# Memory attentions: VectorE subtracts a turned part one step later, behind the next unit's maximum and normalising

## The chip, the cores and the metric

The kernel runs on one core of a Trainium2 chip. Its time is the device time of one execution in microseconds (us), and a change is judged by the medians of several executions. Five engines work side by side, each through its own list of instructions in order: TensorE (PE in the profile; its weight loads are PEld), VectorE (DVE), ScalarE (ACT), GpSimd (POOL) and SyncE (SP). They wait for each other through semaphores.

## The reference

Two transformer blocks on 512 tokens of width 1024. Each of the three layers in them ends with a memory cross attention, which is what the change touches, and a feed-forward part:

```python
def memory_cross_attention(h, m, wq, wkv, wo):
    q = (h @ wq).reshape(b, t, XA_HEADS, XA_HEAD_DIM)          # 4 heads of 256
    k, v = jnp.split(m @ wkv, 2, axis=-1)                      # 256 memory rows
    ...
    s = jnp.einsum("bthd,bmhd->bhtm", q, k).astype(jnp.float32) * (XA_HEAD_DIM ** -0.5)
    p = jax.nn.softmax(s, axis=-1).astype(v.dtype)
    o = jnp.einsum("bhtm,bmhd->bthd", p, v).reshape(b, t, D_MODEL)
    return o @ wo
```

In the first block the same attention stands once, after a mixer of two causal attentions; in the second block it stands once after each of two mixers. That makes three memory attentions: `xa0`, `xa1` and `xa2`.

## The kernel before

All large products are made from float32 operands split in two: a high part (`_hi`, rounded) and the rest (`_lo`, the value less its high part), and a product is three matmuls, high by high, low by high and high by low (L974). ScalarE makes the high parts of activations, VectorE the rests; for weights, GpSimd makes most rests (L820).

A memory attention has 16 **units**: 4 heads by 4 query tiles of 128 tokens, numbered 0 to 15. The work on unit s is spread over the engines:

- TensorE: scores S(s), four float32 matmuls into a bank of the ring `ps_s` (L1381).
- VectorE: the negated row maximum of the scores (L2710, reads `ps_s`).
- ScalarE: the exponential with its row sum (L1975).
- VectorE: reciprocal of the sum (L2486) and the normalising multiply (L2488).
- TensorE: two transposes of the normalised tile, T(s), into a bank of the ring `ps_l` (L1123).
- ScalarE: the high part of the turned tile (L1967). VectorE: its **rest** (L2725), which needs the turned tile and the high part, and gives the bank back.
- TensorE: when a head's four units are turned, its values product in two halves, V(h,0) and V(h,1), six matmuls each (L974 on `vm_hi`). ScalarE takes the high part of the result (L1981), VectorE its rest (L2716), here called P(h,0) and P(h,1).

The order is written out once, by `attention_events`, as a list of events that all engines walk; each takes of it what is its own. In step s stand S(s), then at some steps P, then T(s-3), and V(h,0) at the end of step 4h+8, V(h,1) at the end of step 4h+10. P(h,0) and P(h,1) stand in steps 4h+9 and 4h+11. On VectorE the function `walk` follows the list: at S(s) it makes the maximum of s and then normalises s-1 (at S(15) both 14 and 15), and at T(s-3) it makes the rest of s-3.

What TensorE waits for here: T(s) waits until s is normalised; V(h,·) waits for the rest of unit 4h+3 (`wait_read` on the turned group); and every group of the ring `ps_l` (T and V alike) waits until the group four places earlier has been given back, by a rest or by a P. The order of those groups is T0 to T5, V(0,0), T6, T7, V(0,1), T8, T9, V(1,0), T10, T11, V(1,1), T12, T13, V(2,0), T14, T15, V(2,1), V(3,0), V(3,1).

Of the kernel before, what the change touches and what calls it, by code (L numbers as in the profile page):

```python
# [2 lines left out]

# [14 lines left out]
T = 512  # L18
# [474 lines left out]
def build(nc, A, out):  # L493
    plan = make_plan()
    L, S = plan.L, plan.S
# [17 lines left out]
    def weight(name):  # L513
        name, _, layer = name.partition(":")
        a = A[name]
        return a[int(layer or 0)] if len(a.shape) == 3 else a

    with ExitStack() as ctx:
# [255 lines left out]
        def out_group(t, half):  # L774

            return (L, L.base["ffn1_last"] + t) if half else (S, S.base["out"] + t)
# [193 lines left out]
        def _(pe):  # L970
# [253 lines left out]
            def causal_values(name, rows, vt):  # L1224
                at = plan.events[name][1]

                def values(g, h, _):
                    claim(pe, L, g)
                    wait_read(pe, L, at["T", h, TT - 1])
                    for k in range(TT):  # L1230
                        ins = pe.matmul(bank(L, g)[rows(h), k * P:T], vt(h, k), pt(h)[:, k, k * P:T],
                                        start=k == 0, stop=k == TT - 1)
                    ins.then_inc(l_full, 1)
                return values
# [15 lines left out]
            def pair_values(name, vt):  # L1250
                at = plan.events[name][1]

                def values(g, p, _):
                    claim(pe, L, g)
                    wait_read(pe, L, at["T", p, TT - 1] + 1)
                    for k in range(TT):
                        for e in (0, 1):
                            ins = pe.matmul(bank(L, g)[64 * e:64 * e + 64, k * P:T], vt(2 * p + e, k), pt_row(e, k),  # L1258
                                            start=k == 0, stop=k == TT - 1)
                    ins.then_inc(l_full, 1)  # L1260
                return values
# [1010 lines left out]
        def _(dve):  # L2272
# [74 lines left out]
            for n in range(KD):  # L2347
                g = S.base["x_in"] + n
# [9 lines left out]
            g = S.base["vecs"]  # L2358
# [4 lines left out]
            g = S.base["table"]  # L2363
# [24 lines left out]
            g = S.base["forget"]  # L2388
# [15 lines left out]
            g = S.base["flip"]  # L2404
# [3 lines left out]
            g = S.base["cum"]  # L2408
# [31 lines left out]
            for kind, h, i in ev:  # L2440
                g = at[kind, h, i]
# [36 lines left out]
            def ring_who(g):  # L2478
                return L.who[g]

            def plain_norm(name, exp_done, buf, width, h, i):

                u = TT * h + i
                exp_done(h, i)
                a = u % 8
                step(dve.reciprocal(rl[:, a:a + 1], ls[:, a:a + 1]))  # L2486
                sync()
                dve.tensor_scalar(buf[:, i, 0:width(i)], buf[:, i, 0:width(i)], rl[:, a:a + 1], None, ALU.mult)\  # L2488
                    .then_inc(u_p, 1)

            def walk(name, heads, scores, exp_done, buf, width, values, filled=None, turned=None):
                ev, at = plan.events[name]
                seen, normed = 0, 0
                for kind, h, i in ev:
                    g = at[kind, h, i]
                    upto = normed
                    if kind == "S":
                        scores(g, h, i)
                        upto = seen
                        seen += 1  # L2500
                        if seen == heads * TT:
                            upto = seen
                    done = kind == "G" and ring_who(g) == "v" and h[2] == h[3] - 1
                    if done:
                        upto = seen
                    while normed < upto:
                        plain_norm(name, exp_done, buf, width, *divmod(normed, TT))
                        normed += 1
                    if done:
                        filled(g, *h[0:2])  # L2510
                    if kind == "T" and turned:
                        turned(g, h, i)
                    if kind == "P":
                        values(g, h, i)


            def pair_norm(exp_done, p, i):
# [81 lines left out]
            for n in range(KD):  # L2599
                g = L.base["proj_b"] + n  # L2600
# [88 lines left out]
            def cross(c, k_norm, after):  # L2689
# [29 lines left out]
                def turned_rest(g, h, i):  # L2719
# [6 lines left out]
                        .then_inc(l_free["v"], 1)  # L2726

                walk(name, XA_HEADS, scores, lambda h, i: wait_read(dve, S, at["S", h, i]), p_x, lambda i: MEM, values,
                     turned=turned_rest)
                residual(L.base[f"xo{c}"], after, *([angle_steps()] if c == 1 else []))  # L2730
# [63 lines left out]
            g = S.base["norm4"]  # L2794
# [88 lines left out]
            for q in range(4):  # L2883
                g = L.base["pool_w"] + q
# [19 lines left out]
            g = S.base["ln_mean"]  # L2904
# [128 lines left out]
            g = L.base["dq2"] + 1  # L3033
# [27 lines left out]
            for half in (0, 1):  # L3061
                for j in (0, 1) if not half else (1,):
                    query_turn(half, j)
                g = L.base[f"uk{half}"]
# [20 lines left out]
                for kind, h, i in plan.events[name][0]:  # L3085
                    g = at[kind, h, i]
# [23 lines left out]
            for t in range(TT):  # L3110
# [3 lines left out]
                for half in (0, 1):  # L3114
                    ring, g = out_group(t, half)
# [45 lines left out]
```

## Time and profile before

| | |
|---|---|
| median of 3 runs | 2370.75 us (2370.62 to 2371.77) |
| profiled execution, its own time | 2372.24 us |
| its span on the core | 2370.4 us |
| TensorE busy | 2331.8 us, 98% of the span |
| VectorE busy | 1224.9 us, 52% |
| ScalarE busy | 944.9 us, 40% |
| GpSimd busy | 994.8 us, 42% |

The profile page gives busy times of one execution; the span is what the trace covers. TensorE is nearly always at work, so a microsecond in which it waits is a microsecond of the kernel, wherever it lies. The three memory attentions are 33 us each.

### The profile page before, as it was taken

Reading aid. Unit: us, or ns where it says so; the run is one execution under the profiler, and the core shown is the slowest. Engines: PE = TensorE matmul, PEld = TensorE weight load, DVE = VectorE, ACT = ScalarE, POOL = GpSimd, SP = SyncE. Lnnn points to the kernel's source line nnn. Section 1 sums busy time; section 2 is a strip of 40 time slices with the busy share of each in tenths; the row PEclk is TensorE's granted clock in tenths of the full one; section 3 lists DMA queues with packets and bytes.
Section 4 is the critical chain, followed back from the end, with each engine's and each line's share of the span. In section 5 each row is a group of like instructions: output and inputs, shape, how many; then the busy total and the mean of one; then the engine's idle time right before and its main releaser. Section 6 shows DMA issues by size and latency. Waiting matters only on the chain.

```text
span 2370.4 us, 29903 instructions
## 1 busy us (share of the span) xinstructions
PE 2331.8 (98%) x11132; PEld 1863.8 (79%) x11132; DVE 1224.9 (52%) x2017; ACT 944.9 (40%) x1451; POOL 994.8 (42%) x744
## 2 busy tenths in 40 slices
PE   8999999999999999999999999999999999999999
PEld 6777778878888888857878888887667878888887
DVE  4454546343433436794466555556774343655544
ACT  3345444433332226535344222225875433322222
POOL 4323335223545445535515545444113233545443
PEclk9999999999999999999999999999999999999999
DMA  5222222422232323223222232322013422232231
GB/s 175 71 72 93 92 90 89 160 72 87 96 106 90 103 92 107 90 72 107 71 69 96 93 103 90 101 93 77 29 37 107 160 72 73 97 107 89 88 107 71
DMA packets 170090, 218.74 MB, mean 92 GB/s; under 512 B 6585, under 2 KB 144107, under 8 KB 169975
## 3 DMA queue, kind: packets, MB, share of 16 engines
q1 hardware_dynamic: 168278, 214.59, 27.6%
q10 hardware_dynamic: 1696, 2.61, 0.3%
q8 instruction: 74, 1.21, 0.2%
q14 instruction: 42, 0.34, 0.0%
HBM read 215.05 MB, written 2.12 MB: 92 GB/s over the span
## 4 chain that ended last, share of the span: by engine, by line
PE 88%; DVE 5%; ACT 3%; issue 2%; DMA 1%; POOL 1%; DVEq 0%; SPq 0%; ACTq 0%
PE ps_l L974 81%; PE ps_s L1493 1%; PE ps_l L1123 1%; ACT w_hi L1649 1%; DVE small L3090 1%; POOL w_lo L820 1%; DVE arena L3082 1%; DVE a_lo L2725 1%; DVE small L2710 1%; PE ps_s L1275 0%; PE ps_s L1322 0%; PE ps_s L974 0%; PE ps_l L1622 0%; DVE small L3092 0%; PE ps_l L1258 0%
## 5 line engine op out<-in xcount | busy, mean ns | idle before, releaser
L820 POOL TENSOR_TENSOR w_lo<-w_raw,w_hi 128x512 fp32r<-128x512 f32 (+1 forms) x740 | 994.6, 1376 | 1354.4 <-ACT w_hi L1649 1344.2
L974 PE MATMUL ps_l<-a_hi,w_hi 128*128 128x512 f32 x1936 | 761.6, 393 | 3.7 <-POOL w_lo L820 2.7
L974 PE MATMUL ps_l<-a_lo,w_hi 128*128 128x512 f32 x1952 | 758.9, 389 | 0.0
L974 PE MATMUL ps_l<-a_hi,w_lo 128*128 128x512 f32 x1936 | 754.4, 390 | 0.0
L1649 ACT ACTIVATE w_hi<-w_raw 128x2048 fp32r<-128x2048 f32 (+2 forms) x196 | 370.6, 1891 | 583.0 <-PE ps_l L974 564.7
L974 PEld LDWEIGHTS ps_l<-a_hi,w_hi 128*128 128x128 f32 x1936 | 363.0, 188 | 89.2 <-issue 9.4
L974 PEld LDWEIGHTS ps_l<-a_lo,w_hi 128*128 128x128 f32 x1952 | 366.2, 188 | 77.6 <-issue 2.2
L974 PEld LDWEIGHTS ps_l<-a_hi,w_lo 128*128 128x128 f32 x1936 | 363.1, 188 | 76.9
L974 PE MATMUL ps_l<-b_hi,w_hi 128*128 128x512 f32 (+1 forms) x892 | 329.5, 369 | 5.8 <-issue 2.3
L974 PE MATMUL ps_l<-b_hi,w_lo 128*128 128x512 f32 (+1 forms) x892 | 326.7, 366 | 0.0
L974 PE MATMUL ps_l<-b_lo,w_hi 128*128 128x512 f32 (+1 forms) x892 | 326.7, 366 | 0.0
L974 PEld LDWEIGHTS ps_l<-b_hi,w_hi 128*128 128x128 f32 x892 | 168.1, 189 | 37.0 <-issue 3.9
L974 PEld LDWEIGHTS ps_l<-b_hi,w_lo 128*128 128x128 f32 x892 | 168.2, 189 | 27.4
L974 PEld LDWEIGHTS ps_l<-b_lo,w_hi 128*128 128x128 f32 x892 | 168.2, 189 | 27.2 <-issue 0.2
L2975 DVE TENSOR_TENSOR x_T<-ps_l,x_T 128x512 f32<-128x512 f32 x160 | 109.2, 688 | 44.6 <-PE ps_l L974 42.6
L2769 DVE TENSOR_TENSOR x_T<-ps_l,x_T 128x512 f32<-128x512 f32 x120 | 82.9, 690 | 59.0 <-PE ps_l L974 58.0
L1681 ACT ACTIVATE a_hi<-x_T,cols 128x512 fp32r<-128x512 f32 x64 | 46.2, 723 | 141.5 <-DVE x_T L2658 141.5
L2658 DVE TENSOR_TENSOR x_T<-ps_l,x_T 128x512 f32<-128x512 f32 x64 | 43.5, 687 | 111.6 <-PE ps_l L974 111.2
L2940 DVE TENSOR_TENSOR arena<-ps_l,rst 128x512 f32<-128x512 f32 x44 | 30.4, 692 | 134.3 <-PE ps_l L974 121.2
L2745 DVE SCALAR_TENSOR_TENSOR arena<-ps_l,rst 128x512 f32<-128x512 f32 x32 | 22.0, 691 | 146.6 <-PE ps_l L974 137.3
L2949 DVE SCALAR_TENSOR_TENSOR arena<-arena,cols 128x512 f32<-128x512 f32 x88 | 91.3, 1038 | 8.4 <-DVE arena L2945 0.3
L2958 DVE TENSOR_TENSOR arena<-ps_l,rst 128x512 f32<-128x512 f32 x44 | 30.3, 691 | 125.9 <-PE ps_l L974 125.9
(314 smaller groups left out, 2446.3 us busy)
## 6 DMA issues: line engine op xcount, KB each, us to landing
w_raw<-in_ffn_w_up_dram SPq DMA_DIRECT2D x44, 1024.0 KB, 5.0
w_raw<-in_w_dram SPq DMA_DIRECT2D x32, 1024.0 KB, 5.1
w_raw<-in_ffn_w_down_dram SPq DMA_DIRECT2D x22, 1024.0 KB, 4.9
w_raw<-in_w_in_dram SPq DMA_DIRECT2D x20, 1024.0 KB, 5.3
w_raw<-in_xa_wkv_dram SPq DMA_DIRECT2D x16, 1024.0 KB, 5.3
w_raw<-in_w_kv_mem_dram SPq DMA_DIRECT2D x8, 1024.0 KB, 5.4
w_raw<-in_xa_wq_dram SPq DMA_DIRECT2D x8, 1024.0 KB, 5.0
w_raw<-in_xa_wo_dram SPq DMA_DIRECT2D x8, 1024.0 KB, 5.1
```

Source lines behind the costliest of these rows:

```text
L820: e.tensor_tensor(w_lo[:, b % 2, o], w_raw[:, b % 2, o], w_hi[:, b % 2, o].bitcast(F32), ALU.subtract).then_inc(w_lo_made[by], 1)
L974: ins = pe.matmul(o, *((v, w) if swap else (w, v)), start=first and n == 0, stop=last and n == 2)
L1123: return pe.transpose(o, v, ident)
L1493: ins = pe.matmul(bank(S, g + swapped)[out:out + 64, :], diag(n, j - first)[rows, :], gl[rows, q, j:j + T], start=j < first + 2, stop=j >= ...
L1649: act.activation(w_hi[:, b % 2, 0:size], w_raw[:, b % 2, 0:size], ACT.Copy).then_inc(w_hi_made, 1)
L1681: act.activation(z_of(k)[0][:, n, :], x[:, n, :], ACT.Copy, scale=gain(k, n)).then_inc(n_hi, 1)
L2658: dve.tensor_tensor(x[:, n, :], bank(L, g)[:, :], x[:, n, :], ALU.add).then_inc(l_free["v"], 1)
L2769: dve.tensor_tensor(x[:, n, :], bank(L, g + n)[:, :], x[:, n, :], ALU.add)\
L2940: dve.tensor_tensor(gp[:, c, 2:T + 2], bank(L, g + c)[:, :], rst, ALU.mult)\
L2949: dve.scalar_tensor_tensor(out=cv[:, c, :], in0=gp[:, c, j:T + j], scalar=wcol(cw + 22 * j, k, i), in1=cv[:, c, :], op0=ALU.mult, op1=ALU. ...
L2958: dve.tensor_tensor(f32[:, c, :], bank(L, g + 2 + c)[:, :], rst, ALU.mult)\
L2975: dve.tensor_tensor(x[:, n, :], bank(L, g + n)[:, :], x[:, n, :], ALU.add)\
```

## The change

`walk` no longer makes the rest of a turned part where T stands in the list. It puts it in a queue and makes it at the next S, behind that unit's maximum and the normalising, or, where no S comes, ahead of the next P or T. Only the memory attentions hand `turned` to `walk`; nothing else moves, and no other engine's list changes.

```diff
+import collections
...
                 seen, normed = 0, 0
+                waiting = collections.deque()
                 for kind, h, i in ev:
...
                     if done:
                         filled(g, *h[0:2])
-                    if kind == "T" and turned:
-                        turned(g, h, i)
+                    while waiting and (kind == "S" or kind in "PT" and waiting[0][0] < g):
+                        turned(*waiting.popleft())
                     if kind == "P":
                         values(g, h, i)
+                    if kind == "T" and turned:
+                        waiting.append((g, h, i))
+                while waiting:
+                    turned(*waiting.popleft())
```

In the changed kernel the lines of `walk`'s parts have other numbers: maximum L2716, reciprocal L2487, normalising L2489, rest L2731, P L2722.

VectorE at the first rest of `xa0`, before (rest of unit 0 into bank `ps_l0`, between the normalising of unit 2 and the maximum of unit 4):

```order
L2710 TENSOR_REDUCE small<-ps_s 128x1
L2486 RECIPROCAL small<-small 128x1
L2488 TENSOR_SCALAR arena<-arena,small 128x256
L2725 TENSOR_TENSOR a2_lo<-ps_l0,a2_hi 128x2x128
L2710 TENSOR_REDUCE small<-ps_s 128x1
L2486 RECIPROCAL small<-small 128x1
L2488 TENSOR_SCALAR arena<-arena,small 128x256
L2725 TENSOR_TENSOR a2_lo<-ps_l1,a2_hi 128x2x128
```

and the same place in the changed kernel:

```order
L2716 TENSOR_REDUCE small<-ps_s 128x1
L2487 RECIPROCAL small<-small 128x1
L2489 TENSOR_SCALAR arena<-arena,small 128x256
L2716 TENSOR_REDUCE small<-ps_s 128x1
L2487 RECIPROCAL small<-small 128x1
L2489 TENSOR_SCALAR arena<-arena,small 128x256
L2731 TENSOR_TENSOR a2_lo<-ps_l0,a2_hi 128x2x128
```

The rest of unit 0 now stands behind the maximum of unit 4 and the normalising of unit 3, and so does each later rest behind one more maximum and normalising.

VectorE at the last scores of `xa0`, before (from the rest of unit 11 in `ps_l2` on, with the maximum of unit 15, the normalising of 14 and 15, and P(1,1) in `ps_l3`):

```order
L2725 TENSOR_TENSOR a2_lo<-ps_l2,a2_hi 128x2x128
L2710 TENSOR_REDUCE small<-ps_s 128x1
L2486 RECIPROCAL small<-small 128x1
L2488 TENSOR_SCALAR arena<-arena,small 128x256
L2486 RECIPROCAL small<-small 128x1
L2488 TENSOR_SCALAR arena<-arena,small 128x256
L2716 TENSOR_TENSOR a_lo<-ps_l3,a_hi 128x512
L2725 TENSOR_TENSOR a2_lo<-ps_l0,a2_hi 128x2x128
L2725 TENSOR_TENSOR a2_lo<-ps_l1,a2_hi 128x2x128
```

and in the changed kernel:

```order
L2716 TENSOR_REDUCE small<-ps_s 128x1
L2487 RECIPROCAL small<-small 128x1
L2489 TENSOR_SCALAR arena<-arena,small 128x256
L2487 RECIPROCAL small<-small 128x1
L2489 TENSOR_SCALAR arena<-arena,small 128x256
L2731 TENSOR_TENSOR a2_lo<-ps_l2,a2_hi 128x2x128
L2722 TENSOR_TENSOR a_lo<-ps_l3,a_hi 128x512
L2731 TENSOR_TENSOR a2_lo<-ps_l0,a2_hi 128x2x128
L2731 TENSOR_TENSOR a2_lo<-ps_l1,a2_hi 128x2x128
```

The rest of unit 11, for which V(2,0) waits, has moved behind the maximum of unit 15 and two normalisings; from P(1,1) on the list is the same.

## Rows read from the trace of the kernel before

**Rows 1.** The page: shares of the chain of work that ended last

```profile
PE 88%; DVE 5%; ACT 3%; issue 2%; DMA 1%; POOL 1%; DVEq 0%; SPq 0%; ACTq 0%
```

**Rows 2.** Windows: the first attention, length, busy time by engine, then granted clock

```profile
499.00:532.00 33.00, 30.75 (x146) 23.68 (x145) 24.86 (x72) 19.05 (x56) 5.09 (x4) 1.00 0.14 48
```

**Rows 3.** Timeline of one turn of VectorE's loop: start, duration, engine; idle before

```profile
509.26 0.41 DVE L2710 TENSOR_REDUCE small<-ps_s 128x1 f32<-128x256 f32 x1
...
509.71 0.47 ACT L1975 ACTIVATE arena<-ps_s,small 128x256 f32<-128x256 f32 x1 [0.89 <-DVE small L2710]
509.78 0.35 DVE L2488 TENSOR_SCALAR arena<-arena,small 128x256 f32<-128x256 f32 x1
...
510.18 0.37 ACT L1967 ACTIVATE a_hi<-ps_l 128x256 fp32r<-128x256 f32 x1
...
510.65 0.42 DVE L2725 TENSOR_TENSOR a_lo<-ps_l,a_hi 128x256 fp32r<-128x256 f32 x1 [0.52 <-ACT a_hi L1967]
510.99 0.41 DVE L2710 TENSOR_REDUCE small<-ps_s 128x1 f32<-128x256 f32 x1
...
511.13 0.50 PE L974 MATMUL ps_l<-a_hi,vm_hi 128*128 128x512 f32 x1 [0.44 <-DVE a_lo L2725]
```

**Rows 4.** Timeline of the attention's start: TensorE, GpSimd and VectorE

```profile
499.22 3.61 PE L1381 MATMUL ps_s<-arena 128*128 128x256 f32 x16
...
500.28 0.42 DVE L2710 TENSOR_REDUCE small<-ps_s 128x1 f32<-128x256 f32 x1 [0.17 <-PE ps_s L1381]
...
501.46 5.09 POOL L820 TENSOR_TENSOR w_lo<-w_raw,w_hi 128x512 fp32r<-128x512 f32 x4 [5.53 <-ACT w_hi L1649]
...
504.59 0.84 DVE L2488 TENSOR_SCALAR arena<-arena,small 128x256 f32<-128x256 f32 x1
...
506.32 0.38 DVE L2488 TENSOR_SCALAR arena<-arena,small 128x256 f32<-128x256 f32 x1
```

**Rows 5.** Timeline of TensorE between the first two halves of values

```profile
512.62 1.02 PE L1381 MATMUL ps_s<-arena 128*128 128x256 f32 x4
...
514.57 0.38 PE L1123 MATMUL ps_l<-keep,arena 128*128 128x128 f32 x2
514.71 0.47 PE L974 MATMUL ps_l<-a_hi,vm_hi 128*128 128x512 f32 x1
```

**Rows 6.** Timeline of the attention's end, TensorE

```profile
523.28 1.02 PE L1381 MATMUL ps_s<-arena 128*128 128x256 f32 x4
...
525.08 0.47 PE L974 MATMUL ps_l<-a_hi,vm_hi 128*128 128x512 f32 x1 [0.34 <-DVE a_lo L2725]
...
527.11 0.77 PE L1123 MATMUL ps_l<-keep,arena 128*128 128x128 f32 x4 [0.39 <-DVE a_lo L2716]
527.86 0.47 PE L974 MATMUL ps_l<-a_hi,vm_hi 128*128 128x512 f32 x1
...
529.32 0.39 PE L974 MATMUL ps_l<-a_hi,vm_hi 128*128 128x512 f32 x1
```

**Rows 7.** Timeline of the attention's end, VectorE

```profile
524.51 0.42 DVE L2725 TENSOR_TENSOR a_lo<-ps_l,a_hi 128x256 fp32r<-128x256 f32 x1 [0.52 <-ACT a_hi L1967]
...
526.10 0.35 DVE L2488 TENSOR_SCALAR arena<-arena,small 128x256 f32<-128x256 f32 x1
526.37 0.68 DVE L2716 TENSOR_TENSOR a_lo<-ps_l,a_hi 128x512 fp32r<-128x512 f32 x1
526.97 0.74 DVE L2725 TENSOR_TENSOR a_lo<-ps_l,a_hi 128x256 fp32r<-128x256 f32 x2
```

**Rows 8.** Timeline of the attention's end, ScalarE

```profile
525.30 0.48 ACT L1975 ACTIVATE arena<-ps_s,small 128x256 f32<-128x256 f32 x1 [0.41 <-DVE small L2710]
...
526.75 0.60 ACT L1981 ACTIVATE a_hi<-ps_l 128x512 fp32r<-128x512 f32 x1 [0.33 <-PE ps_l L974]
```

**Rows 9.** Waits of TensorE in the first attention: us in total, times, longest

```profile
PE ps_l L1123 <- DVE arena L2488: 1.1, 3, 0.5
PE ps_l L974 <- DVE a_lo L2725: 0.8, 2, 0.4
```

## The prediction

> **What bounds the kernel now.** I read the page first: 88% of the chain that ended last runs through TensorE, and 5% through VectorE [rows 1]. So the question is only whether TensorE waits less or more inside the three memory attentions. The windows show the first as 33 us with 30.75 us of TensorE's work, at a granted clock of 1.00 [rows 2]; the other two have the same length, the same clock and TensorE busy to within 0.1 us of it. I therefore work out one attention, on the first one's times, and multiply by three.
>
> The timeline of one turn shows what the change aims at. VectorE's maximum starts at 509.26; the exponential behind it 0.45 later, at 509.71; the turned tile's high part 0.47 later, at 510.18; the rest 0.47 later, at 510.65; and the next maximum 0.34 later, at 510.99 [rows 3]. That is a ring of 1.73 us through two engines, and in it VectorE stands idle for 0.52 us ahead of each rest, since ScalarE makes the exponential of the new unit before the high part of the old one. The change opens this ring: the maximum no longer stands behind the rest.
>
> Is this ring what holds TensorE? Only at the attention's start. From the first values product on, two steps of TensorE are scores, turn, scores, turn and half a values product. The row of scores at 512.62 leads to the turn at 514.57 and the next values at 514.71, and V(0,0) itself took from 511.13 to 512.62 [rows 3, 5]: 1.49 + 2.09 = 3.58 us, without a wait, against 2 x 1.73 = 3.46 us for VectorE. TensorE is the slower of the two there. Its waits by the view of waits are 1.1 us for the normalising and 0.8 for rests [rows 9], and the one of 0.39 for P(1,1) [rows 6], 2.3 us in all.
>
> **The change, part by part.** No instruction is added or taken away; 16 rests in each attention move. From the starts in the rows I take these steps of VectorE: maximum to normalising 0.52 (509.26 to 509.78), normalising to the next instruction 0.27 (526.10 to 526.37), rest to the next 0.34, P to the next 0.60 (526.37 to 526.97) [rows 3, 7]. A step without P is then 0.52 + 0.27 + 0.34 = 1.13 us, if nothing is waited for. From the start of a rest to the matmul that waits for it I have two values: 0.48 (510.65 to 511.13) and 0.57 (524.51 to 525.08) [rows 3, 6, 7].
>
> *Term 1, the start, up to V(0,0).* The first place where order matters is the maximum of unit 4. The normalising of unit 2 starts at 504.59 and takes 0.84 us instead of 0.35 [rows 3, 4]; it ends at 505.43. Now the maximum of 4 can start 0.08 before that end (0.35 against a step of 0.27), at 505.35, and the normalising of unit 3 at 505.87. GpSimd is then still in the last of its four L820 instructions (501.46 + 5.09 = 506.55) [rows 4]. The normalising that started at 506.32 took 0.38 and ended 0.15 after GpSimd; the one at 504.59 ended about as long after the third of the four. I take it that the multiply is held until GpSimd's instruction ends, so from 505.87 it lasts to 506.70, just as before. The Trainium skill says the same of the cause, in the "GPSIMD Engine Reference", section "8. Key points": GpSimd shares its SBUF interfaces with VectorE, and they contend when VectorE runs in a two-port mode. The rows carry the number without it.
>
> From there VectorE is free of the ring: rest 0 at 506.62, maxima of 5, 6 and 7 at 506.96, 508.09 and 509.22, then the rest of unit 3 at 509.22 + 0.52 + 0.27 = 510.01. V(0,0) waits for that rest. In the old kernel the rest of unit 3 stood one step earlier in the list, which is why a ring of 1.73 shortened to 1.13 over three steps doesn't give all of 1.8 us. V(0,0) starts 0.48 later, at 510.49, where it was 511.13: **0.64 us gained**. T(4) and T(5) come earlier too but don't set this. If the multiply is not held, it takes 0.35, and V(0,0) comes 0.48 sooner still: 1.12 gained. That is the bound on the other side. With 0.57 instead of 0.48 it is 0.55.
>
> *Term 2, V(0,1), V(1,0) and V(1,1).* With the ring open VectorE catches up with TensorE and waits for its scores. That makes each half of values depend on something new. V(0,1) needs bank and rest of unit 5, V(1,0) the rest of 7, V(1,1) the bank of unit 9; each of these rests now stands in VectorE's step behind the scores that TensorE made just before. From the first row of scores to the maximum that waits for them is 1.06 us (499.22 to 500.28) [rows 4], then 0.52 + 0.27 to the rest, then 0.57 to the matmul: 2.42 us after the scores began. TensorE by itself would be there after 2.09 [rows 5]. So **each of the three waits 0.33 us: 0.99 lost**. With 0.48 it would be 0.24 each, 0.72. The P's between don't add: in their steps they stand behind the rest.
>
> *Term 3, the end.* I count from the start of S(15), 523.28 before. V(2,0) needs the rest of unit 11. It stood ahead of the maximum of 15 and now stands behind the normalising of both 14 and 15, which waits for the exponential of 15. Maximum at 1.06, exponential at 1.51, normalising of 15 at 2.31 (525.30 to 526.10 is 0.80), rest of 11 at 2.58, V(2,0) at 3.15 [rows 3, 4, 7, 8]. Before: 525.08 - 523.28 = 1.80 [rows 6]. That is 1.35 late. Some of it comes back. T(14) used to wait for P(1,1) and started 2.03 after V(2,0); free of waits it follows after 1.46, as V(3,0) follows V(2,1) (527.86 to 529.32). V(2,1) used to start 0.75 after T(14), and without its wait it needs two turns, about 0.37. So V(2,1) is at 3.15 + 1.46 + 0.37 = 4.98, where it was 4.58. V(3,0) needs the rest of unit 15. This now comes out of another queue: P(2,0) stands ahead of it, and waits for ScalarE's high part of V(2,0), which starts 1.67 after V(2,0) (525.08 to 526.75) and takes 0.60 and about 0.10 more until the reader starts [rows 6, 8]. P(2,0) is at 3.15 + 1.67 + 0.70 = 5.52, the two rests behind it at 6.12 and 6.44, and V(3,0) at 7.01. Before it was 6.04: **0.97 lost**. With 0.48 both times it is 0.79.
>
> Sum for one attention: -0.64 + 0.99 + 0.97 = +1.32 us; three times is +4.0. Against the profiled execution that is 2372.24 + 4.0 = 2376.2; this execution lay 1.5 above the median of the runs, so I put it on the median: 2370.75 + 4.0 = 2374.7. Behind V(3,0) nothing is left that could take it up: TensorE goes on into the output product without a wait [rows 6], and the weights' next parts are asked for when TensorE is done with older ones, so they move along.
>
> The bounds: with the multiply not held and 0.48 throughout, -1.12 + 0.72 + 0.79 = +0.39, or +1.2 in all (2371.9). With 0.57 everywhere -0.55 + 0.99 + 0.97 = +1.41, or +4.2 (2375.0).
>
> **The rivals.** I call 0.2% (4.7 us) what a measurement of this kernel can tell from no change.
>
> *Faster.* The ring is the first thing that one sees, and 0.52 us of VectorE's idle time in each turn of it goes [rows 3]. TensorE's waits that could go with it are 2.3 us in one attention [rows 6, 9]; if all went it would be -6.9 us, 2363.9. The Trainium skill speaks for this: "Perfetto Trace Analysis", section "Optimization Strategies", advises to speed up the engines that block TensorE where it waits. By that rule the ring would be the thing to cut and the time would fall. What speaks against it in this kernel is that two of the three kinds of wait are for rests and for a P, that is, for what the change puts later, and that the ring isn't the slower one from V(0,0) on. It decides only if term 3 doesn't come: that is, if V(2,0) didn't need the rest of 11. Its own wait row says it does [rows 6]. Chance 0.07 for more than 4.7 us.
>
> *Slower by over 0.2%.* Term 2's lag is longer than I take it. It is put together from a maximum at the attention's start and a release at its end, and it counts three times in each attention. At 0.26 us above the sum, +1.58 in each attention, the bound is passed; that is 0.09 more for each of the three halves. If VectorE, waking from a wait, takes 0.2 more each time, it is 1.32 + 0.60 = 1.92, +5.8, 2376.5. Nothing in the rows shows such a waking time, but nothing bounds it well either. Chance 0.28.
>
> *The gains pay for the losses.* The multiply isn't held, so that term 1 gives 1.12, and terms 2 and 3 lie near their low ends: +1 to +2 us, 2372.3. It is the low half of my own case.
>
> **How the numbers follow.** Slower by something up to 0.2% is my forecast, with 0.65 for the whole band within 0.2%, nearly all of it on the slow side. Faster 0.07, slower 0.28. The forecast of the likeliest case is 2374.7. For the range, the low end is the case in which gains pay, 1.2, with 0.3 for what runs scatter: 2371.6. The high end is the slow rival's 2376.5.
>
> **What would show it.** V(0,0) at about 11.3 us from the attention's first scores instead of 11.9. No idle time of VectorE ahead of its rests, but before its maxima, waiting for scores. A wait of 0.2 to 0.35 us ahead of V(0,1), V(1,0), V(1,1) on the rest. The longest wait of each attention ahead of V(2,0), 1.7 us by this working, where it was 0.34 in the row [rows 6]; the wait for P(1,1) gone; and a new one of 0.5 us ahead of V(3,0). The exponential and normalising keep their durations. I am wrong if V(2,0) starts less than 2.5 us after S(15), if V(0,0) gains over 1.5 us, or if TensorE's granted clock falls below 1.00 behind the longer wait.

## The result and the profile after

The changed kernel takes **2379.02 us** in the median of 10 runs (2374.81 to 2379.92), the kernel before, run beside it on the same chip, 2371.81 (10 runs, 2370.62 to 2373.09). The ratio is 1.0027, with a 95% interval of 1.0018 to 1.0035: slower, by 7.2 us where 4.0 were forecast, and above the top of the range (2376.5). Two things have to be told apart from here on. The span of the profiled execution grew by 4.0 us (2370.4 to 2374.4), the number that was forecast, though in part by chance, as is shown below; the timed median grew by more. In what follows two executions that were disturbed as a whole, one of e18 (9963 us) and one of the kernel before beside it (3346 us), are left out.

The page of the changed kernel gives the span, the busy times, and the shares of the chain that ended last:

```profile
span 2374.4 us, 29903 instructions
...
PE 2332.0 (98%) x11132; PEld 1864.4 (79%) x11132; DVE 1225.0 (52%) x2017; ACT 945.7 (40%) x1451; POOL 994.3 (42%) x744
...
PE 90%; DVE 4%; ACT 3%; issue 1%; DMA 1%; POOL 1%; SPq 0%; DVEq 0%; ACTq 0%
```

The chain is of the same kind as before [rows 1]. The window of the first attention (its length, then the busy time of each engine, then the granted clock), and TensorE's waits in it (us in total, times, longest):

```profile
498.00:532.30 34.30, 30.86 (x146) 23.73 (x145) 24.51 (x71) 19.30 (x56) 5.10 (x4) 1.00 0.15 50
```

```profile
PE ps_l L975 <- DVE a_lo L2731: 3.0, 3, 1.7
PE ps_l L1124 <- DVE arena L2489: 0.2, 1, 0.2
```

TensorE's work is within 0.1 us that of [rows 2], at the same clock of 1.00. The waits have changed kind: for the normalising 0.2 us where it was 1.1, for rests 3.0 where it was 0.8 [rows 9]. The timeline of TensorE shows where they lie:

```profile
498.68 3.61 PE L1382 MATMUL ps_s<-arena 128*128 128x256 f32 x16
...
509.92 0.50 PE L975 MATMUL ps_l<-a_hi,vm_hi 128*128 128x512 f32 x1 [0.95 <-DVE a_lo L2731]
...
511.42 1.02 PE L1382 MATMUL ps_s<-arena 128*128 128x256 f32 x4
...
513.84 0.47 PE L975 MATMUL ps_l<-a_hi,vm_hi 128*128 128x512 f32 x1
...
523.06 1.02 PE L1382 MATMUL ps_s<-arena 128*128 128x256 f32 x4
...
526.21 0.47 PE L975 MATMUL ps_l<-a_hi,vm_hi 128*128 128x512 f32 x1 [1.69 <-DVE a_lo L2731]
527.66 0.60 PE L1124 MATMUL ps_l<-keep,arena 128*128 128x128 f32 x4
528.02 0.47 PE L975 MATMUL ps_l<-a_hi,vm_hi 128*128 128x512 f32 x1
...
529.97 0.50 PE L975 MATMUL ps_l<-a_hi,vm_hi 128*128 128x512 f32 x1 [0.32 <-DVE a_lo L2731]
...
532.82 0.39 PE L975 MATMUL ps_l<-a_hi,w_hi 128*128 128x512 f32 x1
```

Step by step this is the forecast. V(0,0) starts 11.24 us after the first scores (11.27 was forecast, 11.91 before). V(0,1) starts 2.42 after the first of its two rows of scores (513.84 - 511.42), where TensorE alone needs 2.09 [rows 5]. The wait that was forecast there shows only in these starts; the view names no wait ahead of V(0,1), V(1,0) and V(1,1), and its three for rests (3.0) are those ahead of V(0,0), 0.95, V(2,0), 1.69, and V(3,0), 0.32. V(2,0) starts 3.15 after S(15), behind a wait of 1.69, where it was 1.80 [rows 6]. The wait for P(1,1) is gone, and V(3,0) starts 6.91 after S(15) (7.01 forecast, 6.04 before). From the first scores to the output product, whose first matmul is the last row, it is 34.14 us; before, 32.82. I use this length as the measure of an attention from here on. It doesn't contain the start of the program, and the profiled executions of the changed kernel agree in it to 0.05 us for each attention.

VectorE shows why V(2,0) waits. This is its timeline at S(15) in the changed kernel:

```profile
524.12 0.42 DVE L2716 TENSOR_REDUCE small<-ps_s 128x1 f32<-128x256 f32 x1 [0.94 <-PE ps_s L1382]
...
525.18 0.16 DVE L2487 RECIPROCAL small<-small 128x1 f32<-128x1 f32 x1 [0.17 <-ACT arena L1976]
525.38 0.35 DVE L2489 TENSOR_SCALAR arena<-arena,small 128x256 f32<-128x256 f32 x1
525.65 0.42 DVE L2731 TENSOR_TENSOR a_lo<-ps_l,a_hi 128x256 fp32r<-128x256 f32 x1
```

The rest of unit 11 could have been made over 2 us before: ScalarE's high part of it ended at 523.26 (its row there has 522.89 and 0.37), and VectorE stood idle for 0.94 us ahead of the maximum of unit 15. It now waits for the scores of 15, their exponential and the normalising, none of which it needs.

All three attentions, first scores to output product, in the two profiled executions:

| | `xa0` | `xa1` | `xa2` | sum |
|---|---|---|---|---|
| before | 32.82 | 32.83 | 32.93 | 98.58 |
| after | 34.14 | 34.18 | 34.16 | 102.48 |

Together +3.90 us. That is the trace's part. What is left of 7.2 us doesn't lie in the attentions. Of the rest of the program the traces show two stretches whose length is not fixed. One is what comes ahead of the first attention, which the change doesn't touch: its first scores start between 497.3 us (e11) and 500.4 us (e2) in the profiled executions. The other lies between `xa1` and `xa2`, and the experiments are about it. From `xa0`'s output product to `xa1`'s first scores it is 645.5 or 645.6 us in every trace, and from `xa2`'s output product to the end 412.8. So the 4.0 us between the two spans are 3.9 of the attentions, 0.6 more between `xa1` and `xa2` and an earlier start by 0.5 (498.68 for 499.22 [rows 4]): that the span agrees with the forecast to the last digit is luck, that the attentions do is not.

### The profile page after: what moved, and what is told of

Same layout as the page of the kernel before. It is cut to its first block, busy times and chain, and to the rows that moved or that the text cites. A ratio compares the mean times of both kernels' runs of the same rounds, so it can differ in the third digit from the quotient of the medians.

```text
span 2374.4 us, 29903 instructions
## 1 busy us (share of the span) xinstructions
PE 2332.0 (98%) x11132; PEld 1864.4 (79%) x11132; DVE 1225.0 (52%) x2017; ACT 945.7 (40%) x1451; POOL 994.3 (42%) x744
## 4 chain that ended last, share of the span: by engine, by line
PE 90%; DVE 4%; ACT 3%; issue 1%; DMA 1%; POOL 1%; SPq 0%; DVEq 0%; ACTq 0%
PE ps_l L975 82%; PE ps_s L1494 1%; PE ps_l L1124 1%; ACT w_hi L1650 1%; DVE small L3096 1%; PE ps_s L1382 1%; POOL w_lo L821 1%; DVE arena L3088 1%; PE ps_s L1276 0%; PE ps_s L1323 0%; PE ps_s L975 0%; DVE small L3098 0%; PE ps_l L1623 0%; PE ps_l L1259 0%; PE ps_l L1232 0%
```

## The experiments

Two questions were open: which of the postponed rests costs and which gains, and what makes the timed difference larger than the attentions' lengths. In each table "lengths" is the change of the three lengths together against the kernel before, from the profiled execution, and "time" the median against the median of the kernel before, run beside it on the same chip. There were 11 runs for each kernel, but 10 for e1 and for e18 and 8 for e8. The executions of one kernel scatter by 3 to 7 us, so the median of one experiment is known to 1 or 2 us, and a single surplus of time over lengths no better.

### e1 to e4: the parts of the change

e1 is the changed kernel again. In e2, e3 and e4 only some of the rests are postponed; all others are made where they stood:

```diff
                     if kind == "T" and turned:
-                        waiting.append((g, h, i))
+                        if COND:
+                            waiting.append((g, h, i))
+                        else:
+                            while waiting:
+                                turned(*waiting.popleft())
+                            turned(g, h, i)
```

COND is `TT * h + i in range(0, 3)` (units 0 to 2) in e2, `in (11,)` in e3 and `in range(0, 11)` in e4.

e1. 

> The changed kernel once more, to see the per-execution granted clock on another chip. Order theory alone (TensorE's waits, 1.2 to 1.3 us in each attention): +4 us over the kernel before, about 2376 us, in every execution, with the same granted clock of 0.999 as the profiled execution had. Clock theory (the order's waits, and on top of them a granted clock that falls for a few microseconds in most executions, because of the wait of 1.7 us ahead of V(2,0)): +6 to +8 us, the executions with a mean clock of 0.997 being the slow ones, and the time going up with every thousandth of clock that is missing by about 2 us.

e2. 

> Only the rests of units 0, 1 and 2 of each attention stand one step later, from unit 3 on each rest stands where it stood before. Order theory: the gain of the start without any loss. V(0,0) starts at about 9.7 us after the first maximum where it was 10.85 (the rest of 3 stands in the step ahead), the later halves wait for nothing new, so -1.0 to -1.2 us in each attention and -3.0 to -3.6 us in all, about 2368. Clock theory: the same, since no long wait arises and the clock stays at that of the kernel before. A rival, that TensorE waits for VectorE again at V(0,1) and the gain is lost there: within 1 us of the kernel before.

e3. 

> Only the rest of unit 11 of each attention stands later, behind the maximum of 15 and the normalising of 14 and 15 (the end of the changed kernel alone). Order theory: V(2,0) starts 3.15 us after S(15) instead of 1.80, V(3,0) about 7.0 instead of 6.04: +0.9 to +1.15 us in each attention, +2.7 to +3.4 us in all. Clock theory: the wait of 1.7 us ahead of V(2,0) is here too, so the granted clock is below that of the kernel before in most executions, and the time is +6 us or so.

e4. 

> The rests of units 0 to 10 stand later as in the changed kernel, those of 11 and on where they were (the change without its end). Order theory: -0.6 us at the start, +0.33 us ahead of each of V(0,1), V(1,0) and V(1,1), and the old waits ahead of V(2,0), T(14) and V(2,1) partly taken up by it: -0.1 to +0.4 us in each attention, so -0.5 to +1 us in all. Clock theory: no wait over 1.0 us is left except about 1.0 to 1.3 ahead of V(0,0), so the clock is that of the kernel before, unless waits of that length are enough, and the time is within 1 us of it.

| | lengths | time | ratio |
|---|---|---|---|
| e1, all postponed | +3.98 | +4.99 | 1.0023 [1.0014, 1.0032] |
| e2, units 0 to 2 | -3.62 | -4.29 | 0.9982 [0.9973, 0.9991] |
| e3, unit 11 | +3.07 | +4.29 | 1.0018 [1.0009, 1.0027] |
| e4, units 0 to 10 | -0.62 | +0.65 | 1.0001 [0.9992, 1.0011] |

Each part does what its term says. The starts on TensorE, in us from the first scores of `xa0`, read from the timelines of the seven kernels (e8 and e11 follow below):

| | before | after | e2 | e3 | e4 | e11 | e8 |
|---|---|---|---|---|---|---|---|
| V(0,0) | 11.91 | 11.24 | 10.73 | 11.92 | 11.23 | 11.91 | 10.39 |
| V(0,1) | 15.49 | 15.16 | 14.31 | 15.50 | 15.15 | 15.83 | 13.97 |
| S(15) | 24.06 | 24.38 | 22.88 | 24.08 | 24.37 | 25.06 | 22.55 |
| V(2,0) | 25.86 | 27.53 | 24.68 | 27.23 | 25.59 | 26.28 | 24.34 |
| V(3,0) | 30.10 | 31.29 | 28.91 | 31.00 | 29.92 | 30.61 | 28.58 |
| output product | 32.82 | 34.14 | 31.63 | 33.87 | 32.64 | 33.33 | 31.32 |

e3 holds term 3 alone: V(2,0) comes 3.15 after S(15) with the wait of 1.69 and V(3,0) 6.92, and one attention costs 1.05 (0.97 forecast). Its waits of TensorE are, beside those of before [rows 9]:

```profile
PE ps_l L975 <- DVE a_lo L2736: 2.5, 3, 1.7
PE ps_l L1124 <- DVE arena L2489: 1.1, 3, 0.5
```

e2 shows that the start alone is worth more than the changed kernel gets from it: V(0,0) comes 1.18 earlier, not 0.67, and all of it arrives at the output product (1.19). The difference of 0.51 is the rest of unit 3, which V(0,0) itself waits for and which e2 doesn't postpone.

e4 was the test of my first thought on the surplus, that the clock falls behind the wait of 1.69 us. e4 has no such wait, and still its time lies 1.27 above what its lengths say; with 11 runs that alone is not clear of noise. The traces decide it: the granted clock is 1.00 through all three attentions in the changed kernel and in e3, which have the wait, and e4, which hasn't, was profiled with two falls elsewhere in the program. That thought is refuted.

### e5 to e7, e9 and e10: where in the program the surplus comes from

The granted clock of a whole execution differs from execution to execution of one and the same kernel. Of 148 executions of the kernel before, beside e1 to e18, 20 have 0.997, 15 have 0.998 and 113 have 0.999, with mean times of 2374.16, 2372.47 and 2372.01 us. Of 31 of the changed kernel (after, e1 and e15) 13 have 0.997, 15 have 0.998 and only 3 have 0.999. So the changed kernel loses clock more often. But these shares don't hold the whole surplus. In the two lower classes the changed kernel has 2379.15 and 2377.58 us, 5.0 and 5.1 above the kernel before, where the lengths say 3.9; the changed shares alone, with the means of the kernel before, would give 0.8 us. The number is a blunt measure: it is rounded, and it counts a fall at the very end of the program, which costs no more in one trace than in another (412.8 us from `xa2`'s output product to the end in each). The trace says where the others lie. In windows of 20 us over the whole program the kernel before is below 1.00 only in its last 10 us and in the last mixer, behind `xa1`; these are its windows there:

```profile
1710.00:1730.00 20.00, 17.66 (x97) 12.68 (x96) 10.02 (x28) 13.06 (x28) 6.78 (x7) 1.00 0.16 53
1775.00:1795.00 20.00, 17.19 (x92) 11.57 (x91) 7.83 (x28) 13.31 (x32) 5.01 (x4) 0.91 0.27 95
```

in the changed kernel:

```profile
1710.00:1730.00 20.00, 17.66 (x94) 12.22 (x93) 9.84 (x32) 13.82 (x34) 3.07 (x4) 0.91 0.16 53
1775.00:1795.00 20.00, 16.87 (x103) 11.40 (x102) 11.36 (x40) 14.89 (x37) 4.64 (x4) 1.00 0.14 49
```

and in e15, the changed kernel again (e1's profile is like the first one, with a fall at the first place alone):

```profile
1710.00:1730.00 20.00, 17.66 (x92) 12.43 (x91) 9.15 (x29) 13.41 (x31) 4.01 (x5) 0.91 0.16 53
1730.00:1775.00 45.00, 43.32 (x232) 29.55 (x231) 37.08 (x110) 35.76 (x88) 9.60 (x8) 1.00 0.08 25
1775.00:1795.00 20.00, 17.14 (x90) 10.66 (x89) 10.39 (x37) 13.98 (x34) 4.98 (x4) 0.83 0.06 14
```

There are two places, and in each profiled execution the clock falls at none, one or both of them. The waits of TensorE in this stretch (1700 to 1800, e15) name them:

```profile
PE ps_l L975 <- issue: 2.3, 1, 2.3
PE ps_l L1124 <- DVE a_lo L3110: 2.3, 1, 2.3
```

Both kernels have these two idle times of 2.3 us, of the same length. TensorE's timeline in e15 at the first of them:

```profile
1714.19 0.71 PE L1124 MATMUL ps_l<-keep,arena 128*128 128x128 f32 x5
...
1717.24 0.77 PE L975 MATMUL ps_l<-b_hi,w_hi 128*128 128x512 f32 x1 [2.34 <-issue]
1717.81 0.63 PE L975 MATMUL ps_l<-b_lo,w_hi 128*128 128x512 f32 x1
1718.23 0.63 PE L975 MATMUL ps_l<-b_hi,w_lo 128*128 128x512 f32 x1
```

The matmuls behind the idle time take 0.63 us and start 0.42 apart. Where the clock holds (e16, below) they take 0.39 and start 0.23 apart: that is 1.2 GHz and 2.4 GHz, and the granted clock from 1717.5 to 1720.5 in e15 is 0.50. What comes behind the gap pays for it: the stretch from `xa1`'s output product to `xa2`'s first scores is 713.4 us in the profiled executions without a fall (713.9 in e17), 714.3 to 714.9 in those with one, and 716.1 to 717.4 in those with two (not counting the kernels with 18 filling matmuls, below; e8 has a single but longer fall, with 0.50 from 1779 to 1785, and 716.0). So one fall costs 0.9 to 1.5 us, a longer one 2.6, and two together 2.7 to 4.0. The changed kernel gives the mixer no other work. What differs is that it reaches it 2.6 us later, for the two attentions ahead of it.

e5 and e6 split the change at that place: COND is `name == "xa2"` in e5 and `name != "xa2"` in e6. e7, e9 and e10 leave the rests where they were and only delay one attention of the kernel before, by repeating its first scores (in e7 and e10 of `xa1`, ahead of the last mixer; in e9 of `xa2`, behind it):

```diff
-for d in (0, 1):
+for d in (0, 1) * (4 if c == 1 and not h and not i else 1):
```

with `c == 2` in e9 and 7 for 4 in e10. The repeated matmuls write the same sums again.

e5. 

> The change in the third memory attention alone, behind both stretches of the last mixer in which the traces show the granted clock fall (about 1715 and 1785 us). Order theory: +1.3 us over the kernel before. Clock theory as first put (the wait of 1.7 us ahead of V(2,0) makes the clock fall): a third of the extra, +1.3 + 1. Shift theory (the clock falls in the last mixer in every kernel, where TensorE idles for 2.3 us, and how much depends on when these idle times come in the program): nothing is shifted ahead of them, so the same clocks as the kernel before and +1.3 us, 2374.

e6. 

> The change in the first and second memory attention alone, both ahead of the last mixer. Order theory: +2.7 us. Shift theory: the last mixer comes 2.7 us later as in the changed kernel, so its clocks are those of the changed kernel: most executions at 0.997 or 0.998, +2.7 and 1 to 3 us more, 2376 to 2378.

e7. 

> The kernel before, order untouched, with the first scores of the second memory attention computed four times over instead of once (12 float32 matmuls more, 3 x 0.87 = 2.6 us in which TensorE is busy and nothing else changes). Order theory has no clock in it: +2.6 us, 2375. Shift theory: the last mixer comes 2.6 us later, with TensorE never idle for it, and the clock falls as often as in the changed kernel: +2.6 and 1 to 3 us more. The first clock theory (a long wait) predicts +2.6, as there is none.

e9. 

> The kernel before with the first scores of the third memory attention computed four times over: the same 2.6 us of busy TensorE, but behind the last mixer. Shift theory: the mixer comes when it did, so the clocks are those of the kernel before (0.999 in two of three executions) and the time is +2.6 us, 2375.0. If it is only added work that makes the clock fall more, wherever it stands: +4.4, as with the same delay ahead of the mixer.

e10. 

> The kernel before with the first scores of the second memory attention computed seven times over, 6 x 0.87 = 5.2 us of delay ahead of the last mixer instead of 2.6. If the cost of the falling clock grows with the delay (a warmer or slower chip): +5.2 and 3 to 4 us, 2381. If what counts is where the mixer's idle times come, the extra may be more or less than with 2.6 us, anything from -1 to +3 us around 2377.6, and no larger delay is worse for being larger.

| | lengths | time | time less lengths | executions at 0.997, 0.998, 0.999 and over |
|---|---|---|---|---|
| e5, `xa2` postponed | +1.28 | +0.18 | -1.1 | 1, 0, 10 |
| e6, `xa0` and `xa1` postponed | +2.65 | +5.06 | +2.4 | 7, 2, 2 |
| e7, `xa1` delayed | +2.37 | +4.43 | +2.1 | 4, 2, 5 |
| e9, `xa2` delayed | +2.50 | +3.35 | +0.9 | 0, 3, 8 |
| e10, `xa1` delayed more | +3.97 | +4.68 | +0.7 | 0, 5, 6 |

The surplus goes with time lost ahead of the last mixer (e6, e7), and nothing of the change is needed for it: e7 postpones no rest. Lost behind the mixer (e5, e9) it brings a surplus of at most 0.9. By means in place of medians the five surpluses are -0.4, +1.9, +1.9, +0.8 and +0.4, each good to about 1 us; so those of e6 and e7 are clear of zero, and those of e5, e9 and e10 are not, or barely. But e10 doesn't fit a simple rule: with more delay than e7 it has less surplus, by 1.5 us (95% interval 0.1 to 2.9). A delay changes how often the clock falls, and by these runs not in proportion.

### e12 to e18: taking the idle time away

If falls at the idle times are the surplus, it must go when TensorE isn't idle there. The filled kernels put matmuls into the mixer's gaps, whose results are in a bank that nobody reads before it is written anew:

```diff
+if (h, i) == (7, LATENT_ORDER[0]):
+    spare = at["S", 7, LATENT_ORDER[-1]] + 1
+    claim(pe, S, spare)
+    for _ in range(18):
+        pe.matmul(bank(S, spare)[:, 0:P], ones[:, :], ones[:, :], start=True, stop=True)
```

behind the last turn of each latent attention of that mixer: 18 matmuls in e12 (kernel before), e13 (changed kernel) and e14 (e8), 8 in e16, e17 and e18 (the same three). e15 is the changed kernel once more, run beside e12 to e14 on one chip.

e12. 

> The kernel before, with 18 matmuls of 128 columns on a spare bank of the score ring behind the turn of the last head's first tile, in both halves of the last mixer: TensorE is busy for about 2.0 of the 2.3 us in which it idled, and nobody reads what they write. If its idling is what makes the clock fall: a mean clock of 0.999 to 1.000 in every execution, no fall at 1715 or 1785 us, and about 2369.4 us, 3 below the kernel before, with less scatter. If the clock falls for another reason: 2372 and the old scatter, or more by what the filler delays.

e13. 

> The changed kernel with the same filler in both halves of the last mixer. If the falling clock is the whole of what the attentions do not account for: 2373.4 us, that is +4.0 over the kernel before with filler, clock 0.999 to 1.000. If something else in the changed kernel costs time outside the traces: still 2376 or more, +6 over the kernel before with filler.

e15. 

> The changed kernel once more beside the three with filler: 2377 to 2379 us, with clocks of 0.997 and 0.998 in most executions, or, if the profiled execution is one of those, a trace with the clock falling in both stretches of the last mixer.

e16. 

> The kernel before with 8 filler matmuls in each half of the last mixer, 16 passes of 0.11 = 1.8 us of an idle time of 2.3, so that nothing is delayed. If a rest of 0.5 us of idling doesn't make the clock fall: clock 1.000, no delay, about 2369.4 to 2370 us, 2.5 to 3 below the kernel before. If the fall comes from the light work around the idle time as well: clock 0.998 or 0.999 and 2371 or more.

e17. 

> The changed kernel with the same short filler: +4.0 over the kernel before with short filler, 2373.4 to 2374, clock 1.000.

The filled kernels keep the clock. e16's windows, and its timeline at the first gap:

```profile
1710.00:1730.00 20.00, 19.45 (x115) 14.34 (x113) 9.96 (x31) 13.90 (x31) 5.73 (x7) 1.00 0.15 53
1775.00:1795.00 20.00, 18.70 (x116) 13.75 (x115) 8.81 (x32) 13.99 (x33) 5.02 (x4) 1.00 0.28 95
```

```profile
1714.10 0.71 PE L1123 MATMUL ps_l<-keep,arena 128*128 128x128 f32 x5
1714.65 1.95 PE L1618 MATMUL ps_s<-ones 128*128 128x128 f32 x16
1717.15 0.47 PE L974 MATMUL ps_l<-b_hi,w_hi 128*128 128x512 f32 x1 [0.55 <-issue]
1717.46 0.39 PE L974 MATMUL ps_l<-b_lo,w_hi 128*128 128x512 f32 x1
1717.69 0.39 PE L974 MATMUL ps_l<-b_hi,w_lo 128*128 128x512 f32 x1
```

Each of the 8 fp32 matmuls is two passes in the trace (x16, 1.95 us); an idle time of 0.55 us is left, and no fall follows. The 18 of e12 to e14 take about 4.0 us, twice what was expected, where 2.3 were idle, and delay the mixer by about 3 us; that is the larger part of the 4.6 and 4.8 us by which e12 (2374.04) and e14 (2369.67) lie above their expectations. But they do so in both kernels of a pair. e16 has 2370.30 and e17 2374.44, each some 0.4 above what was expected. No profiled execution of the six filled kernels shows a fall in the mixer, and in their 65 executions the whole clock is never below 0.999.

| pair | lengths | time, median against median |
|---|---|---|
| unfilled: after, e1, e15, against before | +3.90, +3.98, +3.89 | +7.21, +4.99, +5.71 |
| 18 matmuls: e13 against e12 | +3.95 | +3.98 |
| 8 matmuls: e17 against e16 | +4.12 | +4.14 |
| 18 matmuls: e14 against e12 | -4.56 | -4.37 |
| 8 matmuls: e18 against e16 | -4.50 | -3.55 |

With the clock held the change costs what its lengths say, in two independent pairs. That the first two agree to 0.03 us is luck: the filled kernels still scatter by 2 to 3 us, as much as the start of the program does in the traces, and the last pair is 0.95 off. By means over all executions the change costs 4.15 and 3.85 us in the filled pairs, 4.0 together (95% interval 3.5 to 4.5), and 6.6, 5.0 and 5.5 in the unfilled ones, 5.7 together (5.1 to 6.2). So 1.7 us (0.9 to 2.5) go when the gaps are filled; on the one chip that has both it is 5.5 (e15) and 4.15 (e13 against e12). In its median e17 is also 3.2 us or more under every unfilled run of the changed kernel (2374.44 against 2377.64 to 2379.02), though on another chip.

### e8, e11, e14 and e18: the best of the order

From e2 follows a version that must beat both kernels: postpone only what frees the maxima at the start, and don't postpone the rest of unit 3. COND is `in (1, 2)` in e8. Here the rest of unit 0 stays as well, since by term 1 it should cost nothing ahead of a normalising that GpSimd holds up. e11 has `in range(4, 11)`, term 2 alone.

e8. 

> Only the rests of units 1 and 2 of each attention stand one step later. If the normalising multiply is held until GpSimd's instruction ends, the rest of unit 0 fits ahead of it at no cost (the multiply of unit 3 then starts at 6.04 us after the first maximum, takes 0.38 and ends at 6.42, as it also does when it starts at 5.59 and takes 0.84), and V(0,0) comes 0.34 earlier than with units 0 to 2 late: -1.5 us in each attention, -4.5 in all, about 2367.5. If the multiply was merely slow, the rest of 0 ahead of it costs what it gives: -1.1 to -1.2 in each, as with units 0 to 2 late.

e11. 

> Only the rests of units 4 to 10 of each attention stand one step later (the second term alone). Order theory, by the attention's length in the trace: V(0,0) as before at 10.85, then a wait of 0.24 to 0.33 us ahead of each of V(0,1), V(1,0) and V(1,1), less what the waits ahead of V(2,0) (0.43) and before T(14) give back, since VectorE now waits for the scores of 15: +0.4 to +0.6 us for each attention, 33.2 to 33.4 us instead of 32.82. Timed: +1.2 to +1.8 us, and up to 2 more by the clock, since the last mixer comes 1 us later.

e14. 

> The order with only the rests of units 1 and 2 late, and the filler: the quickest of all by both parts. 2369.4 - 4.5 = 2364.9 us, 0.9968 of the kernel before. If the filler does nothing: 2366.6 as without it.

e18. 

> The order with only the rests of units 1 and 2 late, and the short filler: 4.2 to 4.6 below the kernel before with short filler, about 2365 to 2365.5, 0.997 of the kernel before, the quickest version of all.

| | lengths | time | ratio |
|---|---|---|---|
| e8, units 1 and 2 | -4.55 | -5.73 | 0.9975 [0.9965, 0.9986] |
| e11, units 4 to 10 | +1.40 | +2.33 | 1.0008 [0.9999, 1.0017] |
| e14, e8 and 18 matmuls | -4.53 | -2.95 | 0.9986 [0.9977, 0.9995] |
| e18, e8 and 8 matmuls | -4.52 | -5.44 | 0.9977 [0.9967, 0.9986] |

e8 is the fastest in its median, 2366.63 us, and e18 with 2366.75 can't be told from it, so no gain by the filling shows there; 2365 to 2365.5 had been expected. e14 is 4.37 under e12, which has the same filling. The timeline of GpSimd and VectorE at the start of e8 bears on the hold by GpSimd:

```profile
499.91 5.09 POOL L821 TENSOR_TENSOR w_lo<-w_raw,w_hi 128x512 fp32r<-128x512 f32 x4 [5.54 <-ACT w_hi L1650]
...
503.04 0.84 DVE L2489 TENSOR_SCALAR arena<-arena,small 128x256 f32<-128x256 f32 x1
503.91 0.42 DVE L2736 TENSOR_TENSOR a_lo<-ps_l,a_hi 128x256 fp32r<-128x256 f32 x1
504.25 0.41 DVE L2721 TENSOR_REDUCE small<-ps_s 128x1 f32<-128x256 f32 x1
504.59 0.15 DVE L2487 RECIPROCAL small<-small 128x1 f32<-128x1 f32 x1
504.77 0.38 DVE L2489 TENSOR_SCALAR arena<-arena,small 128x256 f32<-128x256 f32 x1
```

With the rest of unit 0 ahead of it, the normalising at 504.77 takes 0.38, where it is 0.84 in e2 and the changed kernel. It ends where it would have ended anyhow, 0.15 after GpSimd's last instruction (505.15 for 505.00), so the step of the rest, 0.34, is free; V(0,0) comes 10.39 after the first scores where e2 has 10.73. The whole traces bear it out: in the kernel before, the changed one and e8, all twelve multiplies of each that start inside one of these GpSimd instructions end 0.15 or 0.16 us after it, whether they take 0.38, 0.81 or 0.84, and the other 36 take 0.35 or 0.36.

e11 shows term 2 by itself. V(0,1), V(1,0) and V(1,1) each come 0.33 later, S(15) together 1.00 later; but the output product only 0.51 later, since V(2,0) then finds its rest ready and starts 1.22 after S(15), where it was 1.80 with its wait [rows 6]. In the changed kernel that credit can't be had: there V(2,0) waits for the postponed rest of 11. That is why e4 (-0.18) and e3 (+1.05) sum to 0.87 for `xa0` and not to the change's 1.32.

## Why the prediction was right about the trace and wrong about the time

*What bounds the kernel, and the ring.* Right. TensorE is the slower one from V(0,0) on. That the ring counts only at the start is shown by e2 and e8, whose whole gain lies ahead of V(0,0), and by e11, where opening it in the middle loses.

*Term 1, 0.64 us gained.* Right: 0.67. The hold by GpSimd, which was argued from two ends of instructions, is now shown by all the multiplies above, and the bound of 1.12 for a multiply that isn't held falls. The multiply of unit 3 in the changed kernel took 0.84 us.

*Term 2, 0.33 three times.* Right: V(0,1) and its two fellows stand 2.42 to 2.43 behind their scores, by this sum 2.42. The slow rival, a longer waking of VectorE from a wait, is refuted: it had the right side but not the cause.

*Term 3, 0.97.* Right in its parts (3.15, the wait for P(1,1) gone, V(3,0) at 6.91 where 7.01 was forecast). e3 has it alone, with the output product 1.05 later; V(3,0) in the changed kernel comes 0.87 later behind S(15) than before (6.91 for 6.04).

*The sum.* 1.32 for one attention; measured 1.32, 1.35 and 1.23. Three times is 3.90 for 4.0.

*The faster rival* is refuted as the prediction argued: the waits for the normalising went, and more came back as waits for rests.

*The failed step* is the last, "2370.75 + 4.0 = 2374.7", and it failed in both of its numbers. The smaller part is the base: 2370.75 was the median of three runs, and ten runs of the same kernel gave 2371.81, so 1.1 us of the 4.3 between forecast and result are there. The larger part is what was added, with "Behind V(3,0) nothing is left that could take it up" and, for the clock, a look at rows of the attentions alone [rows 2]. The +4.0 was put on the timed median as if all else in the program stayed as it was. It holds for the work and not for the clock: the last mixer has two idle times of 2.3 us behind which the clock falls to 1.2 GHz in some executions, and in the changed kernel it did so in more of them. That came to 1.0 to 3.3 us on top of 3.9 in the three timings, and in the filled pairs it is gone. The trace of the kernel before had such a fall already, 0.91 in 1775 to 1795, outside the rows that were read. The prediction did name a clock below 1.00 among what would make it wrong, but expected it behind the new wait of 1.69 us, where no trace has it. So the term that was missing is one that the sum put at nothing: the share of executions with falls, times 0.9 to 1.5 us for one and up to 4.0 for two. Of the 7.2 us in the first timing, 3.9 are the attentions. The rest there, 3.3, was larger than in the repeats (1.0 and 1.8 above the lengths in e1 and e15), and only one of those ten executions was profiled, so how its falls were spread isn't shown.

What stays open: why 2.6 us of shift make the falls more frequent. A delay ahead of the mixer brings the surplus (e6, e7), but a longer one brings less of it (e10), and the start of the first attention moves by 3 us from one profiled execution to another with no change at all ahead of it. The Trainium skill, "TensorE: Matmul & The Clock Gate", section "What's actually happening", says that the chip's look at TensorE's activity runs freely and that the same kernel therefore varies from run to run. The variation is in these runs; none shows its cause.

## What to carry to other kernels

Postponing a piece of work on an engine with idle time is free only for the piece itself: find for each piece who waits for it, and postpone only those whose reader comes late (units 1 and 2 here, -4.6 us by the lengths and -5.7 in the median), not those that the next step on the critical engine needs (unit 3, 0.51 us in each attention; unit 11, 1.05). A small expected difference is read from the length of the stage in the trace first, and the base that it is added to comes from more than three runs; when the timed median shows another number, look at the granted clock of every execution and at idle times of TensorE elsewhere in the program, and hold the clock there to compare two versions fairly.

## What the runs showed of the hardware

An idle time of 2.3 us of TensorE was followed by 1.2 GHz in some executions and by 2.4 GHz in others of one kernel, with nothing in the program to tell them apart; with 1.95 us of small matmuls in it, and 0.55 idle, the clock held in all three profiled executions (e16 to e18). In the memory attention a wait of 1.69 us was not followed by a fall in any profile.

A VectorE multiply by a column that starts while GpSimd runs its tensor_tensor ended 0.15 or 0.16 us after GpSimd's instruction, in all of 36 cases in three traces: started 7.10 us after the attention's first scores (e8) it took 0.38 us, started 6.65 after them (e2 and the changed kernel) it took 0.84, and so it ended at 7.48 and 7.49. VectorE's other instructions there, the maximum (0.41) and the rest (0.42), were not lengthened, so they can be put into that time at no cost.
